# Crossing the heads' halves in every round of the chunk inverses

## The chip, the cores and the metric

The kernel runs on one core of one Trainium2 chip. The metric is the device time of one execution, in microseconds; several executions are taken and their median is given. A profile is one further execution, taken by the hardware profiler.

## The reference, cut to what matters

One decoder layer is computed for a prompt of 528 tokens (16 meta tokens and 512 given) and for 8 short samples of 4 tokens. After a large input projection the layer has two branches; the one at issue is the RWKV-7 branch with 32 heads of 64 columns:

```
def step(S, inp):
    r_t, w_t, k_t, v_t, a_t, b_t = inp
    sa = jnp.einsum('nhvk,nhk->nhv', S, a_t)
    S = S * w_t[:, :, None, :] + sa[..., None] * b_t[:, :, None, :] + v_t[..., None] * k_t[:, :, None, :]
    return S, jnp.einsum('nhvk,nhk->nhv', S, r_t)
```

Unrolled over a chunk of 64 tokens, the rule for `sa` is a triangular system, and the kernel inverts its 64 x 64 matrix for each head and chunk.

## The kernel before, in words

The kernel is a sequence of stages. The stage at issue ("d") makes 16 turns, written out in the program, one for each pair of heads. In each turn TensorE also carries out the input projection for the next pair: the generator `steps` (L365 to L367) gives three 128 x 128 matmuls of 280 columns per step, and `run(n)` puts n such steps into TensorE's order as filling between the parts of the recurrence, so that another engine has time to work in the meantime.

The 560 tokens are cut into 9 chunks (`NC`), chunk 8 being the tail with the samples. Each matrix is 64 x 64, and the two heads h = 0, 1 of the pair lie in partitions 0 to 63 and 64 to 127. A 64 x 64 matmul uses the quarter of the array that is given by the half of its input partitions and the half of its output partitions. Uncrossed, head 0 uses the quarter low to low and head 1 the quarter high to high: the two diagonal quarters. For chunks 0 to 3 (`CROSSED = 4`) the program can lay the heads out the other way round. `half_of(c, h, crossed)` gives the half of a head of a chunk, and `each(b, left, right, signal, crossed)` (L1991) issues one product for all 9 chunks and both heads, 18 matmuls, in the order `CHUNK_ORDER = (4, 0, 5, 1, 6, 2, 7, 3, 8)`, so that an uncrossed chunk and one of the first four alternate; it is one *block* in what follows. Its argument `crossed` is a pair: whether the inputs, and whether the outputs, of chunks 0 to 3 are flipped. With (1, 1) both are, so that those chunks use the diagonal quarters as well, in the other order. With (0, 1) or (1, 0) one of the two is, and those chunks use the other two quarters. Each float32 matmul leaves two records in the trace, so a block has 36. `pair(b, c, n)` places chunks 0 to 3 in PSUM bank b and chunks 4 to 8 in bank b + 1.

The inverse is made in this order. VectorE masks the products into `t_full` (L1801, L1803), takes the 16 x 16 block diagonals `t_d` (L1805) and `n_d` (L1809, four instructions on 64 partitions), writes the first estimate `inv = n_d + identity` (L1811, signal `inv_ready`), changes `t_full` (L1813), makes the low parts of one tile of weights (`split_lo`, L351, two instructions), and adds to `af` (L1817, signal `af_ready`). TensorE squares: block `each(6, t_d, n_d)` after `inv_ready`, `run(2)`, block `each(4, n_d, t_d)` after `af_ready`, `run(3)`. *Round 1* has three blocks in a row, 6, 4 and 2, then `run(4)`; *round 2* has blocks 6 and 2, then `run(4)`; *round 3* has block 2, then `run(3)`. The block into bank 2 is the product `t @ inv` in each of the three. Between rounds ScalarE copies one product from PSUM (L1661), and VectorE copies another in the first two (L1827) and adds the product to the estimate (L1829, `inv += psum`, once per round, the signal is `inv_b`). Then follow two rounds with the full matrix (blocks 6, 4, then 2), which are already issued with (1, 0), (1, 0) and (0, 1). The identity stands in both halves of the tile `eye2`.

Of the kernel before, what the change touches and what calls it, by code (L numbers as in the profile page):

```python
# [25 lines left out]
MUL, ADD, SUB, MIN, MAX = ALU.mult, ALU.add, ALU.subtract, ALU.min, ALU.max  # L26
# [10 lines left out]
C = 64  # L37
NC = 9
# [16 lines left out]
COL_GA = COL_ZB + D  # L55
COL_GB = COL_GA + D
ZW = 1 + TP + NSEQ * (TS + 1)
DV, DS, DG = 49, 11, 5
DED = 2
DCV, DCS, DCG = 66, 24, 3  # L60
DECAY = -0.5 * float(np.exp(-0.5))
# [29 lines left out]
def build(nc, x_prompt, x_sample, state_rwkv, state_shift, state_gla, meta_tokens, norm_pre, w_in, rwkv_mu, rwkv_w0,  # L91
# [3 lines left out]
    with ctx:  # L95
# [3 lines left out]
        def sig(name, per=0):  # L99
            return Signal(ctx, nc, name, per)  # L100
# [47 lines left out]
        def bc(ap, n, axis=1):  # L148

            u = ap.unsqueeze(axis)  # L150
            shape = list(u.shape)
            shape[axis] = n
            return u.to_broadcast(shape)
# [1149 lines left out]
        n_d, t_d, x2, t2, t_full, inv = (ar(NC, C) for _ in range(6))  # L1303
# [9 lines left out]
        gram = ar(NC, 2, P)  # L1313
# [6 lines left out]
        block16 = ar(C)  # L1320
        eye2 = ar(C)
# [24 lines left out]
        inv_mm, inv_a, inv_b, inv_ready = sig("d_inverse_products", 8), sig("d_inverse_scalar", 5), sig("d_inverse_vector", 9), sig("d_inverse_start", 1)  # L1346
# [32 lines left out]
        CROSSED = 4  # L1379
        CHUNK_ORDER = (4, 0, 5, 1, 6, 2, 7, 3, 8)  # L1380

        def pair(b, c, n):

            at = 512 + (c - CROSSED) * C
            return psum[:, b:b + 2, :].rearrange("p b x -> p (b x)")[:, at:at + n * C]
# [13 lines left out]
        with nc.Block() as block:  # L1399
# [316 lines left out]
            def _(dve):  # L1716
                mine, i = v_order, 0
# [11 lines left out]
                def turn_of(i, last=False):  # L1729
                    recount()  # L1730
                    shifted.count = 1
                    mine = v_order
                    tt, stt, ts = dve.tensor_tensor, dve.scalar_tensor_tensor, dve.tensor_scalar
# [38 lines left out]
                    for part, (x, e, out, sign) in enumerate(((kk_t, exc, a_r, -1.0), (r_t, e_t, a_r, 1.0), (a_t, cum, b_k, 1.0), (k_t, cum, b_k, 1.0))):  # L1772
# [3 lines left out]
                        signal = products if part == 3 else mine  # L1776
# [3 lines left out]
                    for half in range(2):  # L1780
                        cols = slice(half * HALF, (half + 1) * HALF)
                        signal = bonus_done if half else mine
# [9 lines left out]
                    for g in range(3):  # L1792
                        dve.wait_ge(gram_done.sem, gram_done.at(i, g + 1))
                        cs, first, n = ((slice(0, 4), 2, 4), (slice(4, 8), 6, 4), (slice(NF, NC), 2, 1))[g]
                        for h in range(2):
                            signal = gram_read if h else mine
# [10 lines left out]
                    for h in range(2):  # L1807
                        for cs, at in ((slice(0, CROSSED), 64 - 64 * h), (slice(CROSSED, NC), 64 * h)):
                            tt(n_d[at:at + 64, cs], gram[0:64, cs, h, 0:C], bc(block16[0:64], cs.stop - cs.start), MUL).then_inc(mine.sem, 1)  # L1809
                            dve.wait_ge(mine.sem, mine.next(i))  # L1810
                    tt(inv, n_d, bc(eye2, NC), ADD).then_inc(inv_ready.sem, 1)  # L1811
                    dve.wait_ge(inv_ready.sem, inv_ready.next(i))
                    tt(t_full, t_full, bc(eye2, NC), SUB).then_inc(mine.sem, 1)  # L1813
                    dve.wait_ge(mine.sem, mine.next(i))
# [5 lines left out]
                    def both(op, signal):  # L1820

                        op(slice(0, NC), lambda b: pair(b, 0, NC).rearrange("p (c t) -> p c t", c=NC)).then_inc(signal.sem, 1)
                        dve.wait_ge(signal.sem, signal.next(i))
                    for n in range(4):
                        dve.wait_ge(inv_mm.sem, inv_mm.at(i, n + 1))
                        if n < 2:
                            both(lambda c, b: dve.tensor_copy((t2, t_d)[n][:, c, :], b(4)), inv_b)  # L1827
                        if n > 0:
                            both(lambda c, b: tt(inv[:, c, :], inv[:, c, :], b(2), ADD), inv_b)  # L1829
                    for half in range(2):  # L1830
                        dve.wait_ge(pd.evacuated.sem, pd.evacuated.at(i, 9 + half))
                        cols = slice(half * HALF, (half + 1) * HALF)
# [57 lines left out]
                    for half in range(2):  # L1890
                        cols = slice(half * HALF, (half + 1) * HALF)
                        signal = centred if half else mine
# [20 lines left out]
                for i in range(NPAIR):  # L1913
                    turn_of(i, last=i == LAST_TURN)

            @block.tensor
            def _(pe):
# [5 lines left out]
                def turn_of(i, last=False):  # L1923
                    mm, tr = pe.matmul, pe.transpose
# [6 lines left out]
                    for n in range(2):  # L1931
                        for half in range(2):
                            m = mm(bank[2 + 2 * n + half][:, 0:HALF], lora_w[n][0:LORA, :], lora[n][:, half * HALF:(half + 1) * HALF],
                                   start=True, stop=True)
# [25 lines left out]
                    for s in range(NSEQ):  # L1960
                        m = tr(bank[6][:, s * C:(s + 1) * C], state8_in[0:C, s, :], ident[0:C, 0:C])
# [5 lines left out]
                    def run(n):  # L1967
                        for _ in range(n):
                            next(fill, None)
# [18 lines left out]
                    def half_of(c, h, crossed):  # L1988
                        return head[1 - h if crossed and c < CROSSED else h]

                    def each(b, left, right, signal=None, crossed=(1, 1)):  # L1991

                        for c in CHUNK_ORDER:
                            for h in range(2):
                                out = pair(b, c, 1)[half_of(c, h, crossed[1])]
                                at = half_of(c, h, crossed[0])
                                m = mm(out, left(c)[at], right(c)[at], start=True, stop=True)  # L1997
                        if signal:
                            m.then_inc(signal.sem, 1)
                    of = lambda x: (lambda c: x[:, c, :])  # L2000
# [14 lines left out]
                    pe.wait_ge(v_read.sem, v_read.at(i, 3))  # L2015
                    pe.sem_inc(waited.sem, 1)
                    each(4, lambda c: a_r[:, c, 0:C], lambda c: eye2, crossed=(0, 1))
                    pe.wait_ge(a8_ready.sem, a8_ready.at(i, 1))
                    pe.sem_inc(waited.sem, 1)

                    for s in range(NSEQ):
                        for h in range(2):
                            m = mm(bank[5][head[h], 5 * C:6 * C], a8g[head[h], 1 + s, :], s8[head[h], s, :], start=(s == 0), stop=(s == NSEQ - 1),
                                   skip_group_check=True)
                    m.then_inc(a_rows_done.sem, 1)
                    pe.wait_ge(gram_read.sem, gram_read.at(i, 2))
                    pe.sem_inc(waited.sem, 1)
                    each(6, lambda c: a_r[:, c, 0:C], lambda c: b_k[:, c, 0:C], t_done, crossed=(0, 1))
                    run(3)
                    pe.wait_ge(gram_read.sem, gram_read.at(i, 3))  # L2030
                    pe.sem_inc(waited.sem, 1)
                    for c in CHUNK_ORDER:
                        for h in range(2):
                            m = mm(pair(2, c, 1)[half_of(c, h, 1)], gram[C:P, c, h, 0:C],
                                   uv[C:P, c, 64 * h:64 * h + 64], start=True, stop=True)
# [5 lines left out]
                    for c in range(NC):  # L2041
                        m = tr(bank[2 + c // 4][:, c % 4 * P:(c % 4 + 1) * P], b_k[:, c, :], ident[:, :])
                    m.then_inc(bk_turned.sem, 1)
                    pe.wait_ge(inv_ready.sem, inv_ready.at(i, 1))
                    pe.sem_inc(waited.sem, 1)
                    each(6, of(t_d), of(n_d))
                    run(2)
                    pe.wait_ge(bk_read.sem, bk_read.at(i, 1))
                    pe.sem_inc(waited.sem, 1)
                    pe.wait_ge(af_ready.sem, af_ready.at(i, 1))  # L2050
                    pe.sem_inc(waited.sem, 1)
                    each(4, of(n_d), of(t_d), inv_mm)
                    run(3)
                    pe.wait_ge(inv_a.sem, inv_a.at(i, 1))
                    pe.sem_inc(waited.sem, 1)
                    pe.wait_ge(inv_b.sem, inv_b.at(i, 1))
                    pe.sem_inc(waited.sem, 1)
                    each(6, of(t2), of(x2))
                    each(4, of(x2), of(t2))
                    each(2, of(t2), of(inv), inv_mm)  # L2060
                    run(4)
                    pe.wait_ge(inv_a.sem, inv_a.at(i, 2))
                    pe.sem_inc(waited.sem, 1)
                    pe.wait_ge(inv_b.sem, inv_b.at(i, 3))
                    pe.sem_inc(waited.sem, 1)
                    each(6, of(n_d), of(t_d))
                    each(2, of(t_d), of(inv), inv_mm)
                    run(4)
                    pe.wait_ge(inv_a.sem, inv_a.at(i, 3))
                    pe.sem_inc(waited.sem, 1)  # L2070
                    pe.wait_ge(inv_b.sem, inv_b.at(i, 4))
                    pe.sem_inc(waited.sem, 1)
                    each(2, of(x2), of(inv), inv_mm)
                    run(3)
                    for n in range(2):
                        pe.wait_ge(inv_b.sem, inv_b.at(i, 5 + 2 * n))
# [13 lines left out]
                    for c in range(NC):  # L2090
                        for h in range(2):
                            m = mm(bank[2 + 3 * h + c // 4][0:C, c % 4 * P:(c % 4 + 1) * P], inv[half_of(c, h, 1), c, :], af[half_of(c, h, 1), c, :], start=True, stop=True)
# [6 lines left out]
                    for c in range(NC):  # L2099
                        k = C if c < NF else TAIL  # L2100
                        for h in range(2):
                            m = mm(bank[2 + c // 4][head[h], c % 4 * P:(c % 4 + 1) * P], p_t[0:k, h, c, :], gram[0:k, c, h, :], start=True, stop=True)
# [3 lines left out]
                    for c in range(NC):  # L2106
                        for h in range(2):
                            right = uv[:, c, 64 * h:64 * h + 64] if c < NF else uv_tail[:, 64 * h:64 * h + 64]
                            m = mm(bank[5 + c // NF][head[h], c % NF * C:(c % NF + 1) * C], gram[:, c, h, 0:C], right, start=True, stop=True)
# [7 lines left out]
                    for c in range(1, NC):  # L2117
# [13 lines left out]
                        for h in range(2):  # L2131
                            before = n_t[head[h], 0, :] if c == 1 else states[head[h], c - 1, :]
                            m = mm(bank[2][head[h], 0:C], m_t[head[h], c, :], before, start=True, stop=True)  # L2133
# [9 lines left out]
                    for s in range(NSEQ):  # L2143
                        at = TAIL + s * TS
                        for h in range(2):
                            m = mm(bank[6][head[h], C + at:C + at + TS], s8[head[h], s, :], a_r[head[h], NF, C + at:C + at + TS], start=False,
                                   stop=(s == NSEQ - 1), skip_group_check=True)
                    m.then_inc(y_state.sem, 1)
                    run(4)
                    for h in range(2):  # L2150
                        pe.wait_ge(uv8_ready.sem, uv8_ready.at(i, h + 1))
                        pe.sem_inc(waited.sem, 1)
                        m = mm(bank[3][head[h], :], gram[:, NF, h, 0:C], uv8[h], start=True, stop=True)
# [26 lines left out]
                for i in range(NPAIR):  # L2180
                    turn_of(i, last=i == LAST_TURN)
# [208 lines left out]
```

## Time and profile before

| | us |
|---|---|
| median of 3 runs | 3309.26 |
| lowest, highest | 3303.74, 3311.22 |
| the profiled execution's own time | 3302.2 |
| its span | 3300.3 |
| TensorE matmul busy (93%) | 3062.6 |
| VectorE busy (52%) | 1713.6 |
| ScalarE busy (32%) | 1057.3 |
| mean granted TensorE clock, share of full speed | 0.966 |

Busy time is the union of the recorded instructions of an engine. Matmuls overlap in the array, so a row that groups many of them gives the time from the first start to the last end, and the time of one matmul can't be had by dividing by the count: the last matmul's own duration is to be taken off first. "PEld" is the load of weights, which runs beside matmuls.

### The profile page before, as it was taken

To read this page: it belongs to the slowest core of one execution; us is meant where nothing else is said; L and a number is where in the kernel's file an instruction comes from. 1 tells how busy PE (TensorE), PEld (TensorE's weight loads), DVE (VectorE), ACT (ScalarE), POOL (GpSimd) and SP (SyncE) were. 2 spreads that over 40 slices of the span, in tenths; PEclk is the share of its full clock that TensorE was granted. 3 is DMA by queue.
4 is the path that set the end of the run, shared out by engine and by line. 5 is a ranking of instruction groups with operands and counts; after the bars stand their busy time and mean duration, and the time that the engine had idled before them with its cause. 6 is when DMAs were issued, how large, how long until landed. Compare 5 with 4: busy or idle time off the path is not lost. (4 is left out here: it accounts for less than half of the span.)

```text
span 3300.3 us, 78107 instructions
## 1 busy us (share of the span) xinstructions
PE 3062.6 (93%) x33143; PEld 2810.9 (85%) x33143; DVE 1713.6 (52%) x2467; ACT 1057.3 (32%) x1688; POOL 393.9 (12%) x804
## 2 busy tenths in 40 slices
PE   2799999999995999999999999999999999994996
PEld 2699798897991899998999999999999999993995
DVE  3244464454543545655664664665664565564224
ACT  3232332332421332432432432332343243242222
POOL 2200100101002210210220220220121021011000
PEclk8899999999996999999999999999999999997998
DMA  3222432424313222321321322222222232123322
GB/s 92 59 78 65 141 99 77 156 65 127 104 39 122 76 56 57 80 66 42 80 67 53 81 65 55 68 67 57 64 71 59 58 80 66 42 66 130 89 76 95
DMA packets 368531, 255.09 MB, mean 77 GB/s; under 512 B 19412, under 2 KB 347600, under 8 KB 366288
## 3 DMA queue, kind: packets, MB, share of 16 engines
q1 hardware_dynamic: 342592, 184.18, 20.4%
q0 software_dynamic: 25600, 66.02, 6.3%
q8 instruction: 258, 4.23, 0.5%
q14 instruction: 81, 0.66, 0.1%
HBM read 212.69 MB, written 37.45 MB: 76 GB/s over the span
## 5 line engine op out<-in xcount | busy, mean ns | idle before, releaser
L365 PE MATMUL psum<-act_hi,w_hi 128*128 128x280 f32 (+3 forms) x5216 | 1594.3, 306 | 76.5 <-DVE w_lo L351 38.7
L367 PE MATMUL psum<-act_hi,w_lo 128*128 128x280 f32 (+3 forms) x5216 | 1524.4, 292 | 0.1
L366 PE MATMUL psum<-act_lo,w_hi 128*128 128x280 f32 (+3 forms) x5216 | 1522.6, 292 | 0.0
L365 PEld LDWEIGHTS psum<-act_hi,w_hi 128*128 128x128 f32 (+2 forms) x5216 | 983.0, 188 | 146.0 <-issue 103.5
L366 PEld LDWEIGHTS psum<-act_lo,w_hi 128*128 128x128 f32 (+2 forms) x5216 | 982.5, 188 | 5.4 <-issue 0.7
L367 PEld LDWEIGHTS psum<-act_hi,w_lo 128*128 128x128 f32 (+2 forms) x5216 | 982.5, 188 | 1.1
L351 DVE TENSOR_TENSOR w_lo<-raw,w_hi 128x1024 fp32r<-128x1024 f32 (+1 forms) x326 | 396.6, 1216 | 309.8 <-ACT w_hi L343 298.0
L343 ACT CAST w_hi<-raw 128x1024 fp32r<-128x1024 f32 (+1 forms) x326 | 339.8, 1042 | 80.2 <-DMA raw<-in_w_in_dram 38.6
L1997 PE MATMUL psum<-arena 64*64 64x64 f32 x9216 | 248.3, 221 | 6.4 <-issue 2.6
L1997 PEld LDWEIGHTS psum<-arena 64*64 64x64 f32 x9216 | 225.2, 134 | 33.7 <-issue 33.7
L1552 POOL DMA_DIRECT2D out_s_rwkv_dram<-arena x128 | 77.6, 614 | 1423.1 <-ACT arena L1698 1423.1
L1630 ACT ACTIVATE arena<-psum 128x280 f32<-128x280 f32 x96 | 38.9, 405 | 308.9 <-PE psum L367 307.3
L1661 ACT COPY arena<-psum 128x576 f32<-128x576 f32 x80 | 51.3, 642 | 230.4 <-PE psum L1997 229.9
L386 ACT COPY arena<-psum 128x248 f32<-128x248 f32 (+1 forms) x50 | 18.3, 367 | 267.7 <-PE psum L367 267.7
L1874 DVE SCALAR_TENSOR_TENSOR arena<-psum,arena 128x64 f32<-128x64 f32 x128 | 36.4, 284 | 115.0 <-PE psum L2133 114.9
L700 ACT COPY arena<-psum 128x280 f32<-128x280 f32 x48 | 18.8, 393 | 235.2 <-PE psum L367 234.9
L2317 DVE COPY arena<-psum 128x256 f32 (+1 forms) x32 | 13.6, 425 | 148.4 <-PE psum L2363 148.4
L1518 POOL DMA_DIRECT2D arena<-in_state_rwkv_dram x128 | 75.1, 604 | 43.9 <-DMA m_dram<-arena 38.4
L1899 DVE RECIPROCAL arena<-arena 128x560 f32<-128x560 f32 x16 | 58.5, 3654 | 37.5 <-ACT arena L1705 37.5
L750 ACT ACTIVATE arena<-psum 128x280 f32<-128x280 f32 x32 | 12.9, 404 | 198.2 <-PE psum L367 198.2
L1829 DVE TENSOR_TENSOR arena<-arena,psum 128x576 f32<-128x576 f32 x48 | 36.2, 755 | 77.0 <-PE psum L1997 76.5
L976 DVE SCALAR_TENSOR_TENSOR arena<-arena,psum 128x512 f32<-128x512 f32 x64 | 47.9, 748 | 51.0 <-PE psum L1257 49.1
(326 smaller groups left out, 3329.4 us busy)
## 6 DMA issues: line engine op xcount, KB each, us to landing
raw<-in_w_in_dram SPq DMA_DIRECT2D x288, 512.0 KB, 4.4
arena<-in_state_gla_dram POOLq DMA_DIRECT2D x32, 512.0 KB, 5.1
out_s_gla_dram<-arena POOLq DMA_DIRECT2D x32, 512.0 KB, 3.3
raw<-in_w_out_dram SPq DMA_DIRECT2D x32, 512.0 KB, 4.5
ob_dram<-arena POOLq DMA_DIRECT2D x16, 280.0 KB, 3.0
arena<-ob_dram POOLq DMA_DIRECT2D x16, 280.0 KB, 4.7
m_dram<-arena POOLq DMA_DIRECT2D x16, 280.0 KB, 2.6
arena<-m_dram SPq DMA_DIRECT2D x4, 1120.0 KB, 12.1
```

Of the source, the lines that this page charges most:

```text
L343: nc.scalar.copy(w_hi[t % 2][:, ks, 0:width], raw[half][:, :, 0:width]).then_inc(self.hi.sem, 1)
L351: eng.tensor_tensor(w_lo[t % 2][:, ks, 0:width], raw[half][:, :, 0:width], w_hi[t % 2][:, ks, 0:width].bitcast(F32), SUB).then_inc(self.lo ...
L365: pe.matmul(out, hi, act_hi[:, k, cols], start=(k == 0), stop=False)
L366: pe.matmul(out, hi, act_lo[:, k, cols], start=False, stop=False)
L367: mm = pe.matmul(out, lo, act_hi[:, k, cols], start=False, stop=(k == KT - 1))
L976: stt(out=sstate[s % 3][:, n, :], in0=sstate[s % 3][:, n, :], scalar=ends[:, n, GN + s:GN + s + 1], in1=bank[4 + n], op0=MUL, op1=ADD).the ...
L1518: pool.dma_start(state8_in[0:C, s, :].rearrange("v (h k) -> v h k", h=2), state_rwkv[0, s, ds(2 * i, 2)].rearrange("h v k -> v h k")).then ...
L1552: pool.dma_start(s_rwkv[0, s, ds(2 * i, 2)].rearrange("h v k -> v h k"), state_out[0:C, s, :].rearrange("v (h k) -> v h k", h=2)).then_inc ...
L1630: nc.scalar.activation(tg[:, half * HALF:(half + 1) * HALF], bank[half][:, 0:HALF], ACT.Tanh, scale=0.5).then_inc(signal.sem, 1)
L1661: nc.scalar.copy(out, pair(b, 0, NC).rearrange("p (c t) -> p c t", c=NC)).then_inc(signal.sem, 1)
L1899: dve.reciprocal(e_t, e_t).then_inc(mine.sem, 1)
L1997: m = mm(out, left(c)[at], right(c)[at], start=True, stop=True)
```

## The change

The products of the three rounds and the two squarings are issued with flipped inputs or outputs alone, (1, 0) or (0, 1), as the later rounds are. The tiles of chunks 0 to 3 thereby change halves with each product. A product `t @ inv` of these chunks comes out in the other half than `inv` lies in, so `inv` can't be added to it elementwise. For these chunks `each(..., keep=True)` issues a second matmul behind the first, with the identity as weights, that adds `inv` in PSUM: 4 chunks, 2 heads and 3 rounds give 24 matmuls more per turn. VectorE then copies chunks 0 to 3 and adds for chunks 4 to 8, two instructions in place of one. The first estimate of chunks 0 to 3 is made afresh from `gram` in the uncrossed layout: two instructions on 64 partitions and one add of the identity, and one add for chunks 4 to 8, in place of one instruction (L1811). The count `DV` follows (49 to 55).

```diff
-                    tt(inv, n_d, bc(eye2, NC), ADD).then_inc(inv_ready.sem, 1)
+                    for h in range(2):
+                        tt(inv[64 * h:64 * h + 64, 0:CROSSED], gram[0:64, 0:CROSSED, h, 0:C], bc(block16[0:64], CROSSED), MUL).then_inc(mine.sem, 1)
+                        dve.wait_ge(mine.sem, mine.next(i))
+                    tt(inv[:, 0:CROSSED], inv[:, 0:CROSSED], bc(eye2, CROSSED), ADD).then_inc(mine.sem, 1)
+                    dve.wait_ge(mine.sem, mine.next(i))
+                    tt(inv[:, CROSSED:NC], n_d[:, CROSSED:NC], bc(eye2, NC - CROSSED), ADD).then_inc(inv_ready.sem, 1)
...
                         if n > 0:
-                            both(lambda c, b: tt(inv[:, c, :], inv[:, c, :], b(2), ADD), inv_b)
+                            dve.tensor_copy(inv[:, 0:CROSSED], pair(2, 0, CROSSED).rearrange("p (c t) -> p c t", c=CROSSED)).then_inc(mine.sem, 1)
+                            dve.wait_ge(mine.sem, mine.next(i))
+                            tt(inv[:, CROSSED:NC], inv[:, CROSSED:NC], pair(2, CROSSED, NC - CROSSED).rearrange("p (c t) -> p c t", c=NC - CROSSED),
+                               ADD).then_inc(inv_b.sem, 1)
+                            dve.wait_ge(inv_b.sem, inv_b.next(i))
...
-                    def each(b, left, right, signal=None, crossed=(1, 1)):
+                    def each(b, left, right, signal=None, crossed=(1, 1), keep=False):
 
                         for c in CHUNK_ORDER:
-                            for h in range(2):
-                                out = pair(b, c, 1)[half_of(c, h, crossed[1])]
-                                at = half_of(c, h, crossed[0])
-                                m = mm(out, left(c)[at], right(c)[at], start=True, stop=True)
+                            for identity in ((False, True) if keep and c < CROSSED else (False,)):
+                                for h in range(2):
+                                    out = pair(b, c, 1)[half_of(c, h, crossed[1])]
+                                    at = half_of(c, h, crossed[0])
+                                    m = mm(out, eye2[at] if identity else left(c)[at], right(c)[at], start=not identity,
+                                           stop=identity or not keep or c >= CROSSED)
...
-                    each(6, of(t_d), of(n_d))
+                    each(6, of(t_d), of(n_d), crossed=(1, 0))
...
-                    each(4, of(n_d), of(t_d), inv_mm)
+                    each(4, of(n_d), of(t_d), inv_mm, crossed=(1, 0))
...
-                    each(6, of(t2), of(x2))
-                    each(4, of(x2), of(t2))
-                    each(2, of(t2), of(inv), inv_mm)
+                    each(6, of(t2), of(x2), crossed=(0, 1))
+                    each(4, of(x2), of(t2), crossed=(0, 1))
+                    each(2, of(t2), of(inv), inv_mm, crossed=(0, 1), keep=True)
...
-                    each(6, of(n_d), of(t_d))
-                    each(2, of(t_d), of(inv), inv_mm)
+                    each(6, of(n_d), of(t_d), crossed=(1, 0))
+                    each(2, of(t_d), of(inv), inv_mm, crossed=(1, 0), keep=True)
...
-                    each(2, of(x2), of(inv), inv_mm)
+                    each(2, of(x2), of(inv), inv_mm, crossed=(0, 1), keep=True)
```

## Rows read from the trace of the kernel before

**Rows 1.** The page's head and first part: span, busy time of the engines.
```profile
span 3300.3 us, 78107 instructions
PE 3062.6 (93%) x33143; PEld 2810.9 (85%) x33143; DVE 1713.6 (52%) x2467; ACT 1057.3 (32%) x1688; POOL 393.9 (12%) x804
```

**Rows 2.** Busy time by stretch: stretch, length, PE, PEld, DVE, ACT, POOL, clock, DMA.
```profile
2380.00:2500.00 120.00, 119.63 (x1562) 111.16 (x1563) 71.05 (x102) 41.68 (x65) 17.44 (x34) 1.00 0.24 64
```

**Rows 3.** Timeline, TensorE, one turn's inverse: start, length, engine, line, shapes, records.
```profile
1992.35 1.26 PE L1997 MATMUL psum<-arena 64*64 64x64 f32 x36
...
1994.29 0.29 PE L367 MATMUL psum<-act_hi,w_lo 128*128 128x280 f32 x1
1994.72 1.26 PE L1997 MATMUL psum<-arena 64*64 64x64 f32 x36
...
1997.27 3.37 PE L1997 MATMUL psum<-arena 64*64 64x64 f32 x108
...
2002.44 2.31 PE L1997 MATMUL psum<-arena 64*64 64x64 f32 x72
...
2006.43 1.26 PE L1997 MATMUL psum<-arena 64*64 64x64 f32 x36
...
2008.98 1.38 PE L1997 MATMUL psum<-arena 64*64 64x64 f32 x72
```

**Rows 4.** One line's instructions, L1997: records, shortest/median/longest in ns.
```profile
L1997 PE MATMUL psum<-arena x9216: 217/218/268, 1142.6 to 2977.7; 64*64 64x64 f32 x197
```

**Rows 5.** Timeline, weight loads, same turn; in brackets the idle time before.
```profile
1994.69 1.16 PEld L1997 LDWEIGHTS psum<-arena 64*64 64x64 f32 x36 [0.33 <-issue]
...
2002.41 2.21 PEld L1997 LDWEIGHTS psum<-arena 64*64 64x64 f32 x72 [0.26 <-issue]
...
2006.43 1.13 PEld L1997 LDWEIGHTS psum<-arena 64*64 64x64 f32 x36 [0.16 <-issue]
```

**Rows 6.** Timeline, VectorE, the same turn.
```profile
1986.51 0.69 DVE L1801 TENSOR_TENSOR arena<-psum,arena 128x512 f32<-128x512 f32 x1 [2.69 <-PE psum L1997]
...
1988.30 1.91 DVE L1809 TENSOR_TENSOR arena<-arena 64x256 f32<-64x256 f32 x4
1990.24 0.76 DVE L1811 TENSOR_TENSOR arena<-arena 128x576 f32<-128x576 f32 x1
1991.04 0.76 DVE L1813 TENSOR_TENSOR arena<-arena 128x576 f32<-128x576 f32 x1
1991.83 2.48 DVE L351 TENSOR_TENSOR w_lo<-raw,w_hi 128x1024 fp32r<-128x1024 f32 x2
1994.35 0.22 DVE L1817 TENSOR_TENSOR arena<-arena,psum 128x64 f32<-128x64 f32 x1
...
2001.54 0.75 DVE L1829 TENSOR_TENSOR arena<-arena,psum 128x576 f32<-128x576 f32 x1
2004.87 0.76 DVE L1829 TENSOR_TENSOR arena<-arena,psum 128x576 f32<-128x576 f32 x1 [2.57 <-PE psum L1997]
2007.82 0.75 DVE L1829 TENSOR_TENSOR arena<-arena,psum 128x576 f32<-128x576 f32 x1 [2.19 <-PE psum L1997]
```

**Rows 7.** One line's instructions, VectorE: shortest/median/longest in ns, shapes.
```profile
L1809 DVE TENSOR_TENSOR arena<-arena x64: 417/453/486, 1146.8 to 2949.3; 64x256 f32<-64x256 f32 x32, 64x320 f32<-64x320 f32 x32
...
L2317 DVE COPY arena<-psum x32: 424/425/425, 3067.8 to 3269.4; 128x256 f32 x28, 128x256 f32<-128x256 f32 x4
```

**Rows 8.** Timeline, TensorE: first matmul behind two idle stretches of earlier stages.
```profile
154.02 0.37 PE L365 MATMUL psum<-act_hi,w_hi 128*128 128x280 f32 x1 [1.85 <-ACT arena L700]
...
414.29 0.39 PE L365 MATMUL psum<-act_hi,w_hi 128*128 128x280 f32 x1 [1.90 <-ACT arena L698]
```

**Rows 9.** Busy time by stretch, behind each of these two.
```profile
154.80:158.20 3.40, 3.40 (x17) 3.40 (x16) 2.12 (x3) 0.00 (x0) 0.00 (x0) 0.50 0.01 3
...
414.20:417.60 3.40, 3.31 (x26) 3.31 (x27) 2.06 (x5) 0.00 (x0) 0.35 (x1) 1.00 0.04 10
```

More of the change, by code:

```diff
@@ L57 @@
 ZW = 1 + TP + NSEQ * (TS + 1)
-DV, DS, DG = 49, 11, 5
+DV, DS, DG = 55, 11, 5
 DED = 2
```

## The prediction

> **What bounds the kernel now.** I read the page's first part, then busy time by stretch for the turns of stage d, then the timeline of TensorE over one inverse, and beside it the timelines of the weight loads and of VectorE. The first part shows TensorE matmul busy for 3062.6 of 3300.3 us and VectorE for about half of it [rows 1]. In a turn it is starker: of 120 us TensorE is busy 119.63 at the full granted clock, VectorE 71.05 and ScalarE 41.68 [rows 2]. So stage d is as long as what TensorE has in its order, plus the short waits between its parts. Less work on TensorE counts in full, unless TensorE then arrives earlier at something that VectorE has not finished.
>
> There is one such place already. The weight loads sat idle 0.33 us before the block at 1994.69, against 0.16 us before the block at 2006.43, which waits for nothing that is late [rows 5]. What ends at that time is VectorE's `af_ready` add (L1817), from 1994.35 to 1994.57; TensorE's matmul starts at 1994.72, 0.15 us after it [rows 3, 6]. VectorE has no gap between 1986.51, when it gets the product for `t_full`, and 1994.57: masks, first estimate, weight split and add follow each other [rows 6]. From the product of `t_full` to the second squaring the turn is bound by VectorE. A second, smaller place is the block of round 2 at 2002.44 (0.26 us idle, and the add of round 1 ends at 2001.54 + 0.75 = 2002.29, again 0.15 us before) [rows 3, 5, 6].
>
> **The price of a block.** The last record of a run takes 0.22 us itself [rows 4], the rest is pitch. A diagonal block: (1.26 - 0.22) / 35 = 29.7 ns per record; the three together: (3.37 - 0.22) / 107 = 29.4 ns; I take 29.5, so a block of 36 costs 1.06 us. Two blocks of the later rounds, which are issued as the changed ones will be: (1.38 - 0.22) / 71 = 16.3 ns, so 0.59 us a block [rows 3]. A crossed block saves 0.47 us. The numbers fit a simple picture: a chunk's two matmuls occupy two quarters for 4 x 29.5 = 118 ns, a slot; nine chunks on the same two quarters need 9 slots (1.06 us), and where chunks of the other two quarters run beside them 5 slots (0.59 us).
>
> A rule of the Trainium skill speaks against this. "TensorEngine Tiling (Array Packing)", section "Gotcha 1: PSUM Pressure", says that different row tiles can't write one PSUM bank at the same time; head 0 and head 1 of one chunk are different row tiles in one bank, so no two matmuls of a chunk would overlap, crossed or not, and the crossing would give nothing. The 72 records in 1.38 us [rows 3] disagree, and the sum goes by them.
>
> **The change part by part, for one turn.**
>
> *Five blocks crossed without the identity* (both squarings, 6 and 4 of round 1, 6 of round 2). The first squaring lies before the `af_ready` wait, which VectorE sets: its 0.47 us only makes TensorE wait longer and counts nothing. Four count: -4 x 0.47 = -1.88 us.
>
> *Three blocks into bank 2 with 8 more matmuls each* (16 records, 24 matmuls a turn). No row shows an identity product behind a crossed one on the same quarters. From below: all 52 records at 16.3 ns, 0.85 us, a saving of 0.21. From above: no overlap at all, 52 x 29.5 = 1.53 us, a loss of 0.47. By slots: D1 A1, then I1 D2, A2, I2 D3, A3, I3 D4, A4, I4 D5 (D a diagonal chunk, A a crossed one, I its identity products, which must follow A on the same two quarters, while the next D may run beside I): 8 slots of 118 ns, 0.94 us. That is one slot less than now. I take it, since the same counting gives both measured blocks: -3 x 0.12 = -0.35 us.
>
> *The first estimate on VectorE.* One instruction of 0.76 us (L1811) with 0.03 us to the next is replaced by four. The two on 64 partitions with 256 elements take 0.42 each, as the shorter of L1809 do, and the longer of L1809, with 320 elements, take 0.486 [rows 7]; four of them with gaps fill 1.91 us [rows 6]. The add on 128 partitions is bounded by 0.22 (64 elements) and 0.76 us (576); per element that gives 0.42 for 256 and 0.49 for 320. Sum 0.42 + 0.42 + 0.42 + 0.49 + 4 x 0.03 = 1.88, less 0.79: +1.09 us. Behind it on VectorE are L1813, the split and the `af_ready` add, with no idle time, so the add ends at 1995.66 in place of 1994.57 and TensorE goes on at 1995.81 in place of 1994.72: +1.09 us on the path. The first squaring itself is not late: `inv_ready` comes at 1991.00 + 1.09 = 1992.09, and with 0.15 us that is before its start at 1992.35.
>
> *The rounds on VectorE.* The add of 0.75 us becomes a copy of 256 elements (0.425 from PSUM [rows 7]), a gap and an add of 320 (0.49): 0.94, so +0.19. In round 1 TensorE already waits for it: +0.19 us. In round 2 the add ends at 2005.63 and TensorE starts at 2006.43: hidden behind the four steps of filling. In round 3 it would end at 2007.82 + 0.75 + 0.19 = 2008.76 and release at 2008.91, TensorE comes at 2008.98: hidden, by 0.07 us; without that cover 0.19 us. These distances hold whatever a block takes, since both engines count from its end. Behind round 3 VectorE waits for ScalarE's gate and weight casts, which hang on TensorE's filling, so the rest of the turn moves as a whole. The weights' DMAs behind the split start 1.09 us later and TensorE comes to that tile a dozen us after; nothing there.
>
> Sum per turn: -1.88 - 0.35 + 1.09 + 0.19 = -0.95 us. All 16 turns have it (L1997 has 9216 records [rows 4], 576 a turn): -15.2 us. The profiled execution took 3302.2 us (span 3300.3 and 1.9 around it), so 3287.0. The median of the runs shown is 7.1 us above the profiled one, and on it the sum gives 3294.
>
> **Rivals.**
>
> *The identity products use up what the crossing of their blocks frees* (D doesn't slip beside I, but beside A): 5 slots and 4 more, as long as now. -0.60 a turn, -9.6 us, 3300. For it: nothing shows the overlap of I and D. Against: they use different quarters and different banks.
>
> *The identity products break the overlap in their blocks* (the other side). Each must add to what the product before it writes at the same addresses; if it waits for it to leave the array, everything behind it in the order waits too. At 29.5 ns a record each of the three blocks costs 1.53 us: -1.88 + 1.09 + 0.19 + 1.42 = +0.82 a turn, +13 us, 3322. It decides from 1.26 us a block on, where 3 x 0.20 eats the 0.60 left. Against it: the two records of one float32 matmul already add into the same addresses at the present pitch.
>
> *The granted clock falls.* TensorE's idle stretch before the second squaring grows: the last filling matmul ends at 1994.29 + 0.29 - 0.47 = 1994.11, the next starts at 1995.81, 1.7 us. After 1.85 us idle the clock was at 0.50 for the stretch from 154.80 on, after 1.90 us idle at 414 it stayed at 1.00 [rows 8, 9]; so neither is excluded. 3.4 us at the lower level cost 1.7 us of TensorE's time. In all 16 turns: +27 - 15 = +12 us, 3321; from 9 turns on nothing is gained; in a handful, about 3302. For: the waits repeat in every turn. Against: the filling on both sides is dense. The Trainium skill ("TensorE: Matmul & The Clock Gate", "What's actually happening") ties the clock to how busy the array has been; the two rows show that a similar idle stretch may go either way.
>
> *VectorE's longer first estimate is hidden after all*: -2.04 a turn, -33 us, 3277. The wait of 0.33 us and VectorE's unbroken chain speak against it.
>
> **Chances and range.** Forecast 0.57; identity uses up its gain 0.13; clock falls in a few turns 0.12, in most 0.07; overlap broken 0.08; estimate hidden 0.03. From the open costs (identity blocks 0.85 to 1.06 us: 3290 to 3300; VectorE's pieces 0.1 us a turn; runs of one kernel 4 us apart from their median) the forecast's own reach is 3286 to 3304. With the few-turn clock case: 3284 to 3308. About 0.2% (6.6 us) can be told from no change: faster takes the forecast, most of the first rival and half of the few turns, 0.70; slower 0.13; within it 0.17.
>
> **What would show it.** Right: the first squaring and the 6 and 4 blocks at about 16.3 ns a record, three 52-record blocks of 0.9 to 1.0 us each (with the closing 0.22 about 1.15), idle weight loads of about 1.9 us before the second squaring and 0.45 before round 2, VectorE unbroken from the `t_full` masks to the `af_ready` add, turns of 118.95 us in place of 119.9. Wrong: blocks with the identity over 1.1 us, a clock below 1.00 within the turns, or a wait before round 3's followers.

## Result and profile after: slower by 0.45%

| | before | changed |
|---|---|---|
| median, us (7 runs each) | 3306.1 | 3320.8 |
| lowest to highest | 3303.4 to 3311.2 | 3316.5 to 3325.9 |
| span of the profiled execution | 3300.3 | 3317.3 |
| 15 turns of stage d, first to last transposes of `b_k` | 1801.0 | 1812.7 |

The ratio is 1.0045, interval [1.0033, 1.0057]. The forecast was 3294, counted from 3309.3, the median of the three runs shown before; the seven runs before give 3306.1, from which the same sum would give 3291. Of the 17 us between the spans 3.5 stand ahead of the first turn, where nothing was changed; 11.7 are in the 15 turns.

The head of the page, and the queue that fetches the instructions (packets, MB, share):
```profile
span 3317.3 us, 79739 instructions
PE 3044.5 (92%) x33911; PEld 2785.0 (84%) x33911; DVE 1737.2 (52%) x2563; ACT 1058.2 (32%) x1688; POOL 392.9 (12%) x804
...
q8 instruction: 263, 4.31, 0.5%
```
TensorE has 768 records more than before, two for each of the 24 x 16 = 384 added matmuls, and 18 us less busy time [rows 1]. So its work did shrink; it waits more. Timeline of TensorE in one turn (start, length, records, in brackets idle time and what ended it), the answer to [rows 3]:
```profile
2119.21 0.80 PE L2007 MATMUL psum<-arena 64*64 64x64 f32 x36
2122.68 0.80 PE L2007 MATMUL psum<-arena 64*64 64x64 f32 x36 [1.70 <-DVE arena L1822]
2124.76 2.26 PE L2007 MATMUL psum<-arena 64*64 64x64 f32 x124
2129.06 1.68 PE L2007 MATMUL psum<-arena 64*64 64x64 f32 x88 [0.29 <-DVE arena L1836]
2132.41 1.16 PE L2007 MATMUL psum<-arena 64*64 64x64 f32 x52
```
The blocks are as counted: 36 records in 0.80 us in place of 1.26, round 1 in 2.26 in place of 3.37, round 2 in 1.68 in place of 2.31, and a block with identity products in 1.16 in place of 1.26. From its first start to its last the 52 records take 1.16 - 0.22 = 0.94 us, the eight slots of the forecast. VectorE in the same turn, the answer to [rows 6]:
```profile
2117.10 0.87 DVE L1812 TENSOR_TENSOR arena<-arena 64x256 f32<-64x256 f32 x2
2118.01 0.43 DVE L1814 TENSOR_TENSOR arena<-arena 128x256 f32<-128x256 f32 x1
2118.47 0.49 DVE L1816 TENSOR_TENSOR arena<-arena 128x320 f32<-128x320 f32 x1
2119.00 0.76 DVE L1818 TENSOR_TENSOR arena<-arena 128x576 f32<-128x576 f32 x1
2119.79 2.49 DVE L351 TENSOR_TENSOR w_lo<-raw,w_hi 128x1024 fp32r<-128x1024 f32 x2
2122.31 0.22 DVE L1822 TENSOR_TENSOR arena<-arena,psum 128x64 f32<-128x64 f32 x1
...
2127.96 0.42 DVE L1834 COPY arena<-psum 128x256 f32<-128x256 f32 x1
2128.42 0.49 DVE L1836 TENSOR_TENSOR arena<-arena,psum 128x320 f32<-128x320 f32 x1
```
From 2117.10 to 2119.00 the first estimate takes 1.90 us where L1811 took 0.80: +1.10. The weight loads sat idle 1.90 us before the second squaring and 0.49 before round 2 (forecast 1.9 and 0.45):
```profile
2122.65 0.69 PEld L2007 LDWEIGHTS psum<-arena 64*64 64x64 f32 x36 [1.90 <-issue]
...
2129.03 1.57 PEld L2007 LDWEIGHTS psum<-arena 64*64 64x64 f32 x88 [0.49 <-issue]
```
A turn in which nothing else happens is therefore shorter, as forecast: turns 3 and 13 (counted from 0) take 119.85 and 119.70 us with one stop inside a block each (what counts as one is said below) of 0.90 and 0.77, so 118.9 to 119.0 without it, against 119.90 before. But the turns are no longer alike. They run from 119.15 to 124.50 us. Two things do that, and neither is in [rows 3] or [rows 6].

*The clock falls.* Three stretches of turn 5 (columns as in [rows 2]) and its round 1:
```profile
1756.00:1759.50 3.50, 1.80 (x45) 1.54 (x44) 2.38 (x4) 0.81 (x3) 0.00 (x0) 1.00 0.46 126
1759.70:1763.00 3.30, 3.30 (x82) 3.04 (x84) 0.19 (x1) 0.06 (x1) 0.00 (x0) 0.50 0.64 168
1763.10:1766.00 2.90, 2.74 (x68) 2.44 (x60) 1.67 (x3) 0.64 (x1) 0.00 (x0) 1.00 0.02 6
```
```profile
1760.83 3.26 PE L2007 MATMUL psum<-arena 64*64 64x64 f32 x124
```
Behind the wait of 1.7 us the granted clock is at the lower level, 1.2 GHz, for 3.4 us, and the round takes 3.26 in place of 2.26 us. In the 16 turns the clock fell 8 times, in the kernel before not once. Seven of the falls begin within 1.4 us of the end of that wait; the eighth, of 6.8 us, begins in turn 14 inside the interruption of 3.1 us (next paragraph), 5.8 us behind the wait. Turns 0, 1 and 5, with a fall and without an interruption in a block, took 120.4, 120.7 (0.27 of it elsewhere) and 120.4 us: 1.5 us a fall.

*TensorE stops inside the blocks*, nearly always at full clock, and with no semaphore to wait for. One such place in round 1, and the fetches of instructions from 2241 to 2246, queue q8 (packets, MB, share):
```profile
2244.73 1.24 PE L2007 MATMUL psum<-arena 64*64 64x64 f32 x59
2247.78 1.32 PE L2007 MATMUL psum<-arena 64*64 64x64 f32 x62 [1.80 <-issue]
```
```profile
q8 instruction: 1, 0.02, 2.2%
```
I call a step of over 0.2 us between two records inside the blocks an interruption. There are 16 in the 16 turns, 15.2 us together (before 2, 0.8 us; the expectation of `add_first` counts the 13 over 0.25 us, 14.5 us). Each of the 11 that last over 0.6 us ends 2.2 to 3.1 us after a fetch began.

The 15 turns then add up: 15 x -0.95 = -14.3; interruptions in blocks +14.6 (less their ordinary pitch); clock 6 x 1.5 and 2.4 for the double fall (what is left of turn 14 without its interruption): +11.4; small stops elsewhere +2.6; less 2.5 of stops before: +11.8, against the 11.7 measured. The 2.4, and the 2.5 of the kernel before (1801.0 less 15 x 119.9), are what is left over in the turns' lengths, so the sum closes in part by how it is made; the experiments test its first three terms one by one.

### The profile page after: what moved, and what is told of

It is laid out like the page before. It is cut to its first block and busy times, and to the rows that moved or that the text cites. A ratio compares the mean times of both kernels' runs of the same rounds, so it can differ in the third digit from the quotient of the medians.

```text
span 3317.3 us, 79739 instructions
## 1 busy us (share of the span) xinstructions
PE 3044.5 (92%) x33911; PEld 2785.0 (84%) x33911; DVE 1737.2 (52%) x2563; ACT 1058.2 (32%) x1688; POOL 392.9 (12%) x804
## 3 DMA queue, kind: packets, MB, share of 16 engines
q8 instruction: 263, 4.31, 0.5%
## 5 line engine op out<-in xcount | busy, mean ns | idle before, releaser
L2007 PE MATMUL psum<-arena 64*64 64x64 f32 x9984 | 213.7, 227 | 45.8 <-DVE arena L1822 27.2
L2007 PEld LDWEIGHTS psum<-arena 64*64 64x64 f32 x9984 | 188.2, 137 | 75.9 <-issue 75.4
L1797 DVE TENSOR_TENSOR arena<-psum,arena 128x512 f32<-128x512 f32 (+1 forms) x96 | 53.7, 559 | 38.8 <-PE psum L1988 35.8
```

What stands on the lines that cost most here:

```text
L1797: tt(gram[:, cs, h, :], bank[first + h][:, 0:n * P].rearrange("p (c t) -> p c t", c=n), bc(causal[:, g // 2, :], n), MUL).then_inc(signal. ...
L2007: m = mm(out, eye2[at] if identity else left(c)[at], right(c)[at], start=not identity, stop=identity or not keep or c >= CROSSED)
```

## Experiments

Where a kernel's output isn't the reference's, its expectation says what it leaves out.

### The two parts alone

`tensor_part` has TensorE's part of the change and VectorE's instructions of the kernel before. Against the changed kernel:
```diff
-                    for h in range(2):
-                        tt(inv[64 * h:64 * h + 64, 0:CROSSED], gram[0:64, 0:CROSSED, h, 0:C], bc(block16[0:64], CROSSED), MUL).then_inc(mine.sem, 1)
...
+                    tt(inv, n_d, bc(eye2, NC), ADD).then_inc(inv_ready.sem, 1)
...
+                            both(lambda c, b: tt(inv[:, c, :], inv[:, c, :], b(2), ADD), inv_b)
```
`vector_part` is the other half: the kernel before with VectorE's part of the change alone, the four instructions of the first estimate, and the copy and the add in each round.

> TensorE's part of the change alone: all products crossed and the identity products, but VectorE's instructions as before (so the first estimate and the sums of chunks 0 to 3 are wrong; its time alone is of use). By blocks and slots the turn saves 0.95 + 1.09 + 0.19 = 2.23 us, -36 us: 3270. Fetch theory: interruptions inside the blocks cost about 14 us as in the changed kernel, 3284. Clock theory: the wait before the second squaring is 0.8 us in place of 1.9, the clock stays at 1.00 in the turns, 3270. Rival (blocks with identity are dear in themselves): 3300 or more.

> VectorE's part of the change alone: the first estimate in four instructions and the sums in two, with TensorE's blocks as before (chunks 0 to 3 wrong). +1.09 us at af_ready and +0.19 in round 1, a turn: +20 us, 3326. Clock theory: the wait is 1.4 us in place of 0.33, and the clock may fall in some turns, up to +13 more: 3326 to 3339. Fetch theory: no interruptions inside the blocks beyond the 1 or 2 of the kernel before, since they are as slow as there.

Measured: `tensor_part` 3288.8, ratio 0.9948 [0.9927, 0.9968]; 19 interruptions, 17.9 us; one fall of the clock. `vector_part` 3329.7, ratio 1.0063 [1.0046, 1.0079]; 2 interruptions, 0.7 us; no fall. Its turn is 121.19 us, +1.29 (forecast for VectorE's part: +1.28). Turn 4 of `tensor_part`, which has no interruption, takes 117.62 us, -2.28 (forecast for TensorE's part: -2.23). So each part is priced as forecast, and the interruptions come with TensorE's part: its blocks are worth 36 us, of which 18 arrive, and the expected 3284 was missed by 5.

### Taking the wait away

`add_first`: VectorE's `af_ready` add goes ahead of the split, and the second half of the split goes behind the first copy of the rounds.
```diff
-                    pd.split_lo(dve, i, mine, 5)
                     dve.wait_ge(af_read.sem, af_read.at(i, 2))
                     tt(af[:, NF, C:P], af[:, NF, C:P], bank[5][:, 5 * C:6 * C], ADD).then_inc(af_ready.sem, 1)
                     dve.wait_ge(af_ready.sem, af_ready.next(i))
+                    pd.split_lo(dve, i, mine, 5, halves=(0,))
...
                             both(lambda c, b: dve.tensor_copy((t2, t_d)[n][:, c, :], b(4)), inv_b)
+                        if n == 0:
+                            pd.split_lo(dve, i, mine, 5, halves=(1,))
```


> The changed kernel, with VectorE's af_ready add moved ahead of the weight split of tile 5, and the second half of that split moved behind the first copy of the rounds. What I read so far from the trace after: clean turns are shorter by 0.95 us as forecast, but (clock theory) the granted clock falls to 0.50 for 3.4 us in about half of the turns after TensorE waits 1.9 us for af_ready, some 13 us in all, and (fetch theory) 13 interruptions of 0.3 to 3.1 us, 14.5 us together, stand inside the small blocks at full clock, each ending 2.2 to 3.1 us after a 16 KB instruction fetch began. Here the wait shrinks from 1.9 to about 0.4 us (ScalarE's bk copies end last, 0.15 us before), so the clock should not fall. Clock theory alone: 3321 - 24 (16 x 1.5 us of wait) - 13 (clock) - 14 (whatever the clock's falls disturb) = 3270. Both theories: 3284, with interruptions of 10 to 18 us left in the blocks. Rival (the longer wait is harmless, the new blocks themselves are dear): over 3297.

`before_add_first`: the same edit in the kernel before.

> Control: the kernel before with the same move of the af_ready add and of half of the split. TensorE's wait before the second squaring is only 0.17 us over the ordinary there, so 0.2 us a turn, -3 us: 3303. All theories agree; if it gains over 8 us, the move does something that I don't see, and the gain of add_first is not the clock's.

Measured: `add_first` 3279.4, ratio 0.9910 [0.9891, 0.9928]; `before_add_first` 3302.6, 0.9987 [0.9976, 0.9998]. The wait before the second squaring of `add_first`:
```profile
1509.20 0.80 PE L2009 MATMUL psum<-arena 64*64 64x64 f32 x36
...
1511.20 0.80 PE L2009 MATMUL psum<-arena 64*64 64x64 f32 x36 [0.23 <-issue]
```
1.70 us of idle TensorE became 0.23. In the 16 turns the clock did not fall once, and 18 interruptions with 11.3 us are still there. So the interruptions do not need the clock's falls, and the falls go with the wait. By the medians the move is worth 41 us in the changed kernel against 4 in the one before; in the 15 turns of the traces it is 36.8 (1812.7 to 1775.9) against 4.8 (1801.0 to 1796.2). `add_first_again`, the same program in more rounds:

> add_first once more, in more rounds, as the version that beats both kernels: 3279 (3275 to 3283), 0.991 of the kernel before. Its interruptions again at the boundaries of the 256-instruction blocks, 8 to 15 us together, and no fall of the granted clock in the 16 turns.

Measured: 3281.2, ratio 0.9921 [0.9906, 0.9937], 21 interruptions with 13.1 us, no fall. It beats both kernels.

### A longer wait

`longer_wait`: in the changed kernel VectorE makes the last add of the first estimate three times.
```diff
+                    for _ in range(2):
+                        tt(inv[:, CROSSED:NC], n_d[:, CROSSED:NC], bc(eye2, NC - CROSSED), ADD).then_inc(mine.sem, 1)
+                        dve.wait_ge(mine.sem, mine.next(i))
                     tt(inv[:, CROSSED:NC], n_d[:, CROSSED:NC], bc(eye2, NC - CROSSED), ADD).then_inc(inv_ready.sem, 1)
```


> The changed kernel with the last add of VectorE's first estimate made three times in place of once (same result), so that af_ready comes 2 x 0.52 = 1.04 us later and TensorE's wait before the second squaring is 3.0 in place of 2.0 us; inv_ready too is late by about 0.9 us, which splits the wait in two. Clock theory: the granted clock falls in more turns than the 8 of 15 of the changed kernel; 12 to 15 of them, each 1.5 us. 3321 + 16 x 1.04 + (4 to 8) x 1.5 = 3344 to 3350. Rival (the clock's falls come from chance or from the interruptions): 8 falls or so, 3338.

Measured: 3343.2, ratio 1.0107 [1.0086, 1.0127], 15 falls in the 16 turns, seven of them of 6.8 us. Idle time of TensorE before the blocks and what ended it (us in all, times), here and in the changed kernel:
```profile
  DVE arena L1825: 28.8, 16
  DVE arena L1819: 14.2, 16
```
```profile
  DVE arena L1822: 27.2, 16
```
That is 1.8 and 0.9 us a turn here, 1.7 us there, 15 and 8 falls. With 19.8 us in 16 turns (1.2 us a turn) `vector_part` had no fall, `tensor_part` with 9.6 us (0.6) one, right behind an interruption of 2.2 us, and `add_first` none. The clock theory stands; what the falls lacked in one turn and had in the next at the same wait of 1.7 us stays open.

### Where the interruptions stand

TensorE's instructions can be numbered in the order of the trace, those of its queue included, and for each interruption that gives the number of the instruction behind it. In all kernels of this study together there are 143 interruptions inside the blocks, and all 143 times that number lies 28 or 29 beyond a multiple of 256: one and the same place in 256 instructions. At 64 bytes each, 256 instructions are the 16,384 bytes of a packet of queue q8 (4.31 MB / 263), and in the 15 turns of the changed kernel there are 192 such places and 192 packets. A turn has 3276 instructions, which is no multiple of 256, so in each turn these boundaries lie elsewhere. `aligned_low` and `aligned_high` are `add_first` with semaphore increments that pad the turn to 3328 = 13 x 256. In `aligned_high` the 100 is 0.
```diff
-                    fill = pd.steps(pe, i, 2)
+                    left = [100 if i == 0 else 52]
+
+                    def padded(steps):
+                        for _ in steps:
+                            for _ in range(min(left[0], 2 if i == 0 else 1)):
+                                pe.sem_inc(waited.sem, 1)
+                                left[0] -= 1
+                            yield
+                    fill = padded(pd.steps(pe, i, 2))
...
-                    fill = pd.steps(pe, i, 3)
+                    fill = padded(pd.steps(pe, i, 3))
```


> add_first, with 52 semaphore increments more in TensorE's order per turn, one each in the filling steps of tiles 2 and 3 (100 in the first turn), so that a turn has 3328 = 13 x 256 TensorE instructions in place of 3276 and every turn lies alike against the 256-instruction (16,384 byte) blocks in which its program is fetched. Here the blocks begin at matmuls 4, 130, 257, 384, 510 and 636 behind the first transpose of b_k, as in turn 3 of add_first, where the interruptions came to 0.1 us (0.9 us in the same turn of the changed kernel). Fetch theory: no two turns differ, interruptions of 0.1 to 0.5 us a turn in place of 1.0: 3279 less 8 to 14, plus what the increments cost (nothing if the filling hides them, up to 0.03 us each, 1.5 us a turn): 3266 to 3290, the difference to aligned_high is what counts. Rival (the interruptions come from the weights' transfers or from chance): turns differ as before, 3279 and up.

> The same, without increments in the first turn, so that the blocks begin at matmuls 53, 180, 307, 433 in every turn, as in turn 0 of add_first, where interruptions at 180 and 307 came to 1.2 us (0.94 and 0.76 us in the two turns that lie nearly so). Fetch theory: an interruption at matmul 307 (and some at 180) in all 16 turns, 0.8 to 1.2 us a turn, so 8 to 18 us over aligned_low at the same number of instructions. Rival: no difference to aligned_low.

Measured: 3278.0, ratio 0.9898 [0.9874, 0.9922], and 3279.6, ratio 0.9918 [0.9901, 0.9934]. `aligned_low` has 13 interruptions, 8.6 us, all at matmul 636 behind the first transpose, in turn after turn. Three turns:
```profile
1303.71 0.68 PE L2017 MATMUL psum<-arena 64*64 64x64 f32 x27
1304.79 0.35 PE L2017 MATMUL psum<-arena 64*64 64x64 f32 x9 [0.40 <-issue]
...
1421.78 0.68 PE L2017 MATMUL psum<-arena 64*64 64x64 f32 x27
1423.01 0.35 PE L2017 MATMUL psum<-arena 64*64 64x64 f32 x9 [0.56 <-issue]
...
2012.03 0.68 PE L2017 MATMUL psum<-arena 64*64 64x64 f32 x27
2013.16 0.35 PE L2017 MATMUL psum<-arena 64*64 64x64 f32 x9 [0.45 <-issue]
```
The block breaks behind its 27th record each time. `aligned_high` has 28, at matmuls 180, 307 and 433 of its turns, 14.8 us. So the place is the boundary of a fetched block. The sizes were off: `aligned_low` was expected to have next to nothing at matmul 636 and lost 0.5 to 0.9 us there in each of 13 turns, and the 15 turns of the two kernels differ by 5.9 us (1770.9 and 1776.8) where 8 to 18 were expected. The medians, 1.6 apart, don't tell the two apart. Two turns of `aligned_low`, 4 and 9, have no interruption and take 117.45 us each.

The traces also say what TensorE waits for. Each boundary has one packet that begins around it, from 3.0 us before TensorE passes it to 9.9 us after. At none of the 2286 boundaries in the 15 turns of the twelve traces did TensorE pass the *next* boundary less than 2.16 us after that packet began. So the packet brings the block behind the next boundary, and a stop comes where it began late and TensorE used up the block in between sooner. All 76 interruptions over 0.6 us end 2.2 to 3.1 us after their packet began. Eight short ones, of 0.2 to 0.4 us, end 3.5 us or more after it, and for these the cause stays open. In `aligned_low` the packet at issue begins 22.6 to 23.1 us behind the first transpose in the 13 turns with an interruption and 20.6 us in turns 4 and 9, while the weights' transfer (q1) of each of these turns starts at about 18.6. From 20.5 to 22.0 us, turn 1 and turn 4:
```profile
q1 hardware_dynamic: 635, 0.32, 87.0%
```
```profile
q1 hardware_dynamic: 643, 0.32, 85.7%
q8 instruction: 1, 0.02, 4.3%
```
In turn 1 the packet begins at 22.6, as the transfer ends (22.9); the 16th turn has no such transfer and no interruption. Of those 76 interruptions 72 wait for a packet that began during a transfer of weights or as one ended; of all 2286 packets 552 did. That the transfer holds the packet back is argued from this, not shown: no run moves the transfer.

### Fewer instructions, and a thinner stretch

`no_identity`: `add_first` with `for identity in ((False,))`, each product closed by itself (`stop=True`).

> add_first without the identity products (24 matmuls a turn fewer; the estimate of chunks 0 to 3 is left incomplete). By the records a block with them takes 0.94 us from first to last start and one without 0.58: -1.07 us a turn, -17 us, 3262. With 3180 instructions a turn the fetch blocks fall elsewhere, and the runs of small matmuls in a row are shorter (108, 72, 36 records in place of 124, 88, 52) but as fast: interruptions of 5 to 15 us in all, 3256 to 3268. Rival (the identity products are the dear part and stand behind the interruptions): under 3250.

Measured: 3261.1, ratio 0.9858 [0.9836, 0.9881]; undisturbed turns take 116.44 us, 1.0 us less; 11 interruptions, 4.4 us. The identity products cost 16 us in the 16 turns, where their records show 17, not more, and some interruptions go with them.

`spread`: the instructions of `add_first`, but with filling between the blocks.
```diff
                     each(6, of(t2), of(x2), crossed=(0, 1))
+                    run(1)
                     each(4, of(x2), of(t2), crossed=(0, 1))
+                    run(1)
                     each(2, of(t2), of(inv), inv_mm, crossed=(0, 1), keep=True)
...
                     each(6, of(n_d), of(t_d), crossed=(1, 0))
+                    run(1)
                     each(2, of(t_d), of(inv), inv_mm, crossed=(1, 0), keep=True)
...
-                    run(20)
+                    run(17)
```


> add_first with one filling step between the blocks of round 1 (two places) and of round 2 (one place), taken from the late run(20), which becomes run(17). The instructions and their number stay the same, 3276 a turn; only the fast stretch is thinned. Each place costs 0.30 us more of changes between small and large matmuls (148 + 220 ns in place of 50, by the gaps), +0.9 us a turn. Fetch theory (TensorE empties the fetched instructions in the fast stretch): the interruptions inside the blocks shrink from 11.3 us to under 5, so the time is 3279 + 14 - 7 = 3286 (3281 to 3292). Rival (each block boundary has its price whatever the pace): interruptions stay at 9 to 13 us, time 3290 to 3296.

Measured: 3297.6, ratio 0.9966 [0.9954, 0.9978]. There is not one interruption in a block, in 16 turns; 13 of the 15 turns take 118.99 to 119.09 us, so none hides elsewhere either. This settles the fetch theory against "each boundary has its price": 76 boundaries lie inside blocks (84 in `add_first`) and none costs anything. The two closest boundaries are passed 4.1 us apart, as in the kernel before; in `add_first` it is 3.4. The time is above my 3281 to 3292 (and above the rival's range too), as the spreading itself cost 1.56 us a turn (119.01 against 117.45) in place of 0.9. Round 1 and the third place:
```profile
1518.93 0.80 PE L2009 MATMUL psum<-arena 64*64 64x64 f32 x36
1520.24 0.80 PE L2009 MATMUL psum<-arena 64*64 64x64 f32 x36
1521.55 1.16 PE L2009 MATMUL psum<-arena 64*64 64x64 f32 x52
...
1528.58 0.37 PE L365 MATMUL psum<-act_hi,w_hi 128*128 128x280 f32 x1 [0.38 <-ACT arena L1630]
```
In round 1 a block starts every 1.31 us; less the 0.58 of its 36 records and the 0.385 of the step that is 0.34 us a place, 0.30 expected. The rest is a new wait: at 1528.58 TensorE starts 0.68 us behind its last matmul in place of 0.13, 0.55 lost, since with three steps more it reaches tile 5's first step, which needs bank 0, before ScalarE has emptied it. 3 x 0.34 + 0.55 = 1.57. One turn (121.58 us) has a fall of the clock, at 1327, outside the inverse.

## Why the prediction was wrong

- *Price of a block, slots, identity products*: right. 16.3 ns a record, 0.94 us for 52. The rival in which the identity products break the overlap is refuted by the 1.16 us row, and the one in which they use up the gain by 1.16 against 1.26. The rule on one PSUM bank that the prediction weighed from the Trainium skill ("TensorEngine Tiling (Array Packing)", "Gotcha 1: PSUM Pressure") is not what the trace shows: the newly crossed blocks too run at 16 to 17 ns a record (124 in 2.26 us).
- *VectorE's first estimate and rounds*: right, +1.10 and about +0.2; `vector_part` gives 1.29 together, forecast 1.28.
- *Sum of an undisturbed turn*: right, -0.95 forecast, -0.9 to -1.0 measured.
- *The step that failed* is the first one: "less work on TensorE counts in full, unless TensorE then arrives earlier at something that VectorE has not finished". TensorE also needs its instructions. Round 1 now uses 248 instructions in 2.0 us, where it used 216 in 3.2, and so reaches the next boundary before the block behind it is there: +14.6 us over 15 turns, in none of my terms or rivals. The packets begin late in the kernel before too (up to 9.4 us behind a boundary, 8.6 in the changed one); what is new is that TensorE needs them sooner (the closest two boundaries are 3.5 us apart, 4.1 before). `spread`, with the same instructions and none of this, shows that it is the pace.
- *The clock rival* was right in its mechanism and price (1.7 us estimated, 1.5 measured) and got too little weight. I put it at nothing in the sum, and gave 0.12 to a few turns and 0.07 to most of them; it was half, 11.4 us in 15 turns. By itself it would have left -14.3 + 11.4 = -2.9 us, which can't be told from no change. It took both losses, 26 us, to turn -14.3 into +11.7.

The result lies outside the range of 3284 to 3308, whose upper end took in a handful of falls and nothing else. The rivals that gave 3321 and 3322 came close to the number, but neither is what happened: the blocks keep their overlap, and the clock fell in half of the turns, not in all.

## What to carry to other kernels

Where a long wait and small matmuls meet, look at what the wait does to the clock, not at its length alone: moving one 0.22 us add ahead of a 2.5 us weight split (and half of the split further back) was worth 4 us in the kernel before and 41 us in the changed one, 3279 to 3281 us in all. Before making unrolled small matmuls faster, count TensorE's instructions over the densest stretch, and see how soon it comes from one boundary of 256 to the next; a queue that shows 0.5% busy may still be what the engine waits for. Such a stop shows as idle time inside one line's run with "issue" as its reason, at a different place in each turn.

## What the runs showed of the hardware

TensorE's instructions come in packets of 16,384 bytes, one for each 256 that it uses, one block ahead. In the turns of all kernels two packets never began less than 3.3 us apart, and TensorE never passed a boundary less than 2.16 us after the packet for it began. With small matmuls on four quarters it would use up 256 instructions in 2.1 us (an estimate, 128 records at 16.3 ns); with the filling around them two boundaries came as close as 3.4 us. The Trainium skill ("Runtime: NRT & Kernel Launch", "Instruction fetch mechanics") gives the same block of 256 instructions, and the trace agrees; it calls the cost of a boundary mostly hidden, which held for the kernel before (0.8 us), `vector_part` (0.7) and `spread` (none) and not for the kernels with crossed blocks in a row (4.4 to 17.9 us), so the measurement decides. An idle stretch of 1.2 us a turn brought no fall of the clock in 16 turns, 1.7 us brought 8 (one of them with an interruption behind it), and 0.9 with 1.8 brought 15. What stays open: why some packets begin late, and whether moving the weights' transfers would cure it; and why the clock falls in one turn and not in the next at the same wait.
